# A two-block transformer forward pass on one core: GpSimd waits between its pieces, and the first stage's order changes

## What is computed

```
h = x @ w_in                    # 1024 x 2768: q_a, c_kv, q_idx, k_idx, w_idx, q_b, k_b, v_b, f_in
log_f = log_sigmoid(f_in + b_f);  cum_f = cumsum(log_f)
idx   = q_idx . k_idx                            # 8 index heads
score = sum_h w_idx[h] * relu(idx[h])            # causal, then top_k(64) per row
la = q_lat . c_kv[sel] + bias(t5_bucket)         # attention A, 8 heads, over the chosen keys
lb = q_b . k_b + cum_f[query] - cum_f[key]       # attention B, 8 heads, causal
y = concat(softmax(la) . c_kv @ w_uv, softmax(lb) . v_b) @ w_o
```

## Time and profile before

| | |
|---|---|
| median of 3 runs | 1362.13 us (1362.07 to 1362.14) |
| profiled execution | 1362.14 us, of which span 1360.8 us |
| PE busy | 1337.3 us, 98% |
| DVE busy | 1020.5 us, 75% |
| ACT busy | 783.5 us, 58% |
| POOL busy | 148.8 us, 11% |
| mean granted clock of TensorE | 0.998 |

### The profile page before, as it was taken

One profiled execution on the slowest core, in us unless ns is written; L12 is line 12 of the kernel. 1 busy time (PEld: TensorE's weight loads), 2 busy tenths in 40 slices (PEclk: granted clock), 3 DMA queues, 4 the chain that ended last, 5 costly groups with the idle time before them and its releaser, 6 DMA issues. The chain is left out here.

```text
span 1360.8 us, 20748 instructions
## 1 busy us (share of the span) xinstructions
PE 1337.3 (98%) x8197; PEld 1160.1 (85%) x8197; DVE 1020.5 (75%) x1681; ACT 783.5 (58%) x1268; POOL 148.8 (11%) x131
## 2 busy tenths in 40 slices
PE   7999999999999999999999999999999999999998
PEld 6987888888898788887986888888789998888887
DVE  5766478777896788778788677666567997786765
ACT  5644266665443565554677566555557875655553
POOL 4770300000100000000000000000302224000000
PEclk9999999999999999999999999999999999999999
DMA  8622165655563456553542255555344345455551
GB/s 302 244 78 124 65 228 209 242 198 188 193 243 129 182 190 227 196 196 124 211 167 96 97 214 215 216 188 191 148 158 183 127 154 186 151 190 204 193 197 72
DMA packets 38175, 242.17 MB, mean 178 GB/s; under 512 B 4416, under 2 KB 6848, under 8 KB 10688
## 3 DMA queue, kind: packets, MB, share of 16 engines
q1 hardware_dynamic: 38080, 240.86, 48.0%
HBM read 236.89 MB, written 2.64 MB: 176 GB/s over the span
## 5 line engine op out<-in xcount | busy, mean ns | idle before, releaser
L319 DVE TENSOR_TENSOR wlo<-raw,whi 128x2048 fp32r<-128x2048 f32 (+1 forms) x179 | 401.2, 2246 | 103.0 <-ACT whi L296 100.9
L296 ACT ACTIVATE whi<-raw 128x2048 fp32r<-128x2048 f32 x195 | 370.3, 1903 | 82.5 <-PE ps L471 40.0
L408 PE MATMUL ps<-XS,whi 128*128 128x512 f32 x1392 | 331.8, 390 | 0.0
L408 PEld LDWEIGHTS ps<-XS,whi 128*128 128x128 f32 x1392 | 257.8, 188 | 52.1 <-issue 0.6
L460 PE MATMUL ps<-whi,MS 128*128 128x512 f32 x960 | 233.5, 391 | 0.0
L460 PEld LDWEIGHTS ps<-whi,MS 128*128 128x128 f32 x960 | 177.5, 188 | 35.8 <-issue 0.4
L413 PEld LDWEIGHTS ps<-XS,wlo 128*128 128x128 f32 x1392 | 178.5, 191 | 6.8
L413 PE MATMUL ps<-XS,wlo 128*128 128x256 f32 x1392 | 180.6, 283 | 0.0
L388 PE MATMUL ps<-XS,whi 128*128 128x256 f32 x672 | 167.8, 290 | 0.0
L389 PE MATMUL ps<-XS,whi 128*128 128x256 f32 x672 | 164.1, 284 | 0.0
L304 POOL TENSOR_TENSOR wlo<-raw,whi 128x512 fp32r<-128x512 f32 x90 | 125.0, 1421 | 192.9 <-ACT whi L296 104.9
(11 more groups left out here) (330 smaller groups left out, 1543.8 us busy)
## 6 DMA issues: line engine op xcount, KB each, us to landing
raw<-in_up SPq DMA_DIRECT2D x88, 1024.0 KB, 4.8
raw<-in_down SPq DMA_DIRECT2D x44, 1024.0 KB, 4.9
raw<-in_hg_t SPq DMA_DIRECT2D x16, 1024.0 KB, 4.8
raw<-in_od_t SPq DMA_DIRECT2D x8, 1024.0 KB, 5.6
raw<-in_ev_a SPq DMA_DIRECT2D x6, 1024.0 KB, 9.7
raw<-in_wa_o SPq DMA_DIRECT2D x6, 1024.0 KB, 5.1
raw<-in_hg_o SPq DMA_DIRECT2D x6, 1024.0 KB, 4.8
raw<-in_ev_o SPq DMA_DIRECT2D x4, 1024.0 KB, 5.8
```

The costliest lines, as they stand in the source:

```text
L296: ac.activation(parts_of(m)[0][:, 0:w], raw[m % NRAW][:, 0:w], ACT.Copy).then_inc(w_hi)
L319: ve.tensor_tensor(lo[:, c], r[:, c], hi[:, c].bitcast(F32), ALU.subtract).then_inc(w_lo_v)
L408: pe.matmul(banks[i][:, 0:512], hi[:, c], XS[:, k, 0:512], start=(k == 0), stop=False)
```

## The change

GpSimd: between two pieces of 512 columns it now waits until the one before is complete (`pp`, a semaphore of its own), and before the first piece of a tile until its previous tile's low part is complete.

First stage: TensorE takes ev_a 3 between the index heads 0 to 3 and 4 to 7. ScalarE makes the high part of ev_a 5 between the Relus of heads 3 and 4, and that of ev_a 6 behind the Relu of head 7, where that of ev_a 5 was. The copies of L1403 and L1405 go from VectorE to ScalarE (`cum_rows_act`), one pair behind the copies of ev_a 4 (j = 0) and one behind those of ev_a 5 (j = 1). ScalarE waits there for the zero fills of KX (`e_zk`), of QX (`e_zq`) and for the running sum (`e_sn`). TensorE waits for 4 of `e_cum` and 4 of `e_own` before attention.

```diff
--- before.py
+++ after.py
@@ -299,10 +299,16 @@
             if m in PLACE and POOLT[m]:
                 r, (hi, lo), w = raw[m % NRAW], parts_of(m), SCHED[m][2]
                 po.wait_ge(w_hi, PLACE[m] + 1)
-                for a in range(0, w // 2 if SHARED[m] else w, 512):
+                if LOP[m] > 1:
+                    po.wait_ge(w_lo_p, LOP[m] - 1)
+                n = w // 2 if SHARED[m] else w
+                for a in range(0, n, 512):
+
+                    if a:
+                        po.wait_ge(pp.sem, pp.n)
                     c = slice(a, a + 512)
                     ins = po.tensor_tensor(lo[:, c], r[:, c], hi[:, c].bitcast(F32), ALU.subtract)
-                ins.then_inc(w_lo_p)
+                    ins.then_inc(w_lo_p if a + 512 == n else pp.up())
 
         def low_part_dve(m):
             if m in PLACE and (not POOLT[m] or SHARED[m]):
@@ -1103,6 +1109,7 @@
         ea, ev_, eb, ec, eo = FIRST["ev_a"], FIRST["ev_v"], FIRST["ev_b"], FIRST["ev_c"], FIRST["ev_o"]
         E0 = MS0["even"]
 
+        e_zk, e_zq, e_sn, e_own = mark("e_zk"), mark("e_zq"), mark("e_sn"), mark("e_own")
         AT_QB, AT_KB, AT_QA, AT_VB, AT_CT = [6, 8, 10, 12], [7, 9, 11, 15], [16, 17, 17, 18], 14, 5
 
         def x_ready(k):
@@ -1127,7 +1134,8 @@
                 ins = pe.transpose(bank[7][:, 16 * tt:16 * tt + 16], FW[0:16, 128 * tt:128 * tt + 128], ident[0:16, 0:16])
             ins.then_inc(e_fw.up())
             for h in range(0, 8, 2):
-
+                if h == 4:
+                    project(ea + 3, bank[4])
                 pe.wait_ge(e_ac.sem, 3 + h // 4)
                 if h >= 4:
                     pe.wait_ge(e_re.sem, h - 2)
@@ -1141,7 +1149,6 @@
                         ins = pe.matmul(bank[(h + r) % 4][:, a:b], QI[q, c:c + 128], KI[q, 0:b - a], start=True, stop=True)
                         if tt == 1:
                             ins.then_inc(e_ix.up())
-            project(ea + 3, bank[4])
             project(ea + 4, bank[5])
             project(ea + 5, bank[6])
             pe.wait_ge(e_wi.sem, 1)
@@ -1152,7 +1159,8 @@
             accumulate([ev_ + 1], XS, [4, 5, 6, 7], 512, acc, no_wait, False, True)
             pe.wait_ge(e_ac.sem, 6)
             project(eb, bank[4])
-            pe.wait_ge(e_cum.sem, 8)
+            pe.wait_ge(e_cum.sem, 4)
+            pe.wait_ge(e_own.sem, 4)
             pe.wait_ge(cb_in.sem, 1)
             for i in range(-2, 22):
                 if 0 <= i < 16:
@@ -1256,6 +1264,21 @@
                 pe.matmul(ePAIR[p % 2][64 * r:64 * r + 64, 0:256], WV[:, 64 * (h + r):64 * (h + r) + 64], OA[r], start=True,
                           stop=True).then_inc(e_po.up())
 
+        def cum_rows(r):
+            a = 64 - 64 * r
+            own = lambda p: ident[p:p + 8, p:p + 8].rearrange("p (c r) -> p c r", r=2)[:, :, r:r + 1].to_broadcast([8, 4, 256])
+            row = lambda ap: ap.unsqueeze(1).to_broadcast([8, 4, 256])
+            return a, a + 32, own, row
+
+        def cum_rows_act(r):
+
+            a, b, own, row = cum_rows(r)
+            ac.wait_ge(e_zk.sem, 2)
+            ac.activation(hx4(KX, r)[a:a + 8], own(a), ACT.Copy).then_inc(e_own.up())
+            ac.wait_ge(e_zq.sem, 2)
+            ac.wait_ge(e_sn.sem, 1)
+            ac.activation(hx4(QX, r)[a:a + 8], row(FW[a:a + 8, :]), ACT.Copy).then_inc(e_own.up())
+
         def even_act():
             def out_of(m, i, dst, scale=1.0):
                 ac.wait_ge(w_done, DONE[m])
@@ -1285,11 +1308,13 @@
                 ac.wait_ge(w_done, DONE[ea + 1 + j])
                 ac.activation(QI[:, 512 * j:512 * j + 512], bank[5 + j][:, :], ACT.Copy, scale=0.125).then_inc(e_ac.up())
             for h in range(8):
+                if h == 4:
+                    act_weights(ea + 5)
                 ac.wait_ge(e_ix.sem, h + 1)
                 if h >= 2:
                     ac.wait_ge(e_sc.sem, 2 * h - 2)
                 ac.activation(RR[h % 2], bank[h % 4][:, 0:384], ACT.Relu).then_inc(e_re.up())
-            act_weights(ea + 5)
+            act_weights(ea + 6)
             z = slice(0, 104)
             ac.wait_ge(e_fz.sem, 1)
             ac.wait_ge(e_fw.sem, 1)
@@ -1306,6 +1331,8 @@
                 act_weights(ea + 6 + j)
                 heads_of(ea + 4 + j, 0, KX, j)
                 heads_of(ea + 4 + j, 1, QX, j + 1, 0.125)
+                if j < 2:
+                    cum_rows_act(j)
             act_weights(ev_ + 3)
             for tt in range(2):
                 ac.wait_ge(w_done, DONE[ev_ + 1] - 1 + tt)
@@ -1348,7 +1375,7 @@
         def even_dve():
             ve.wait_ge(m_tp.sem, 4)
             for r in range(2):
-                ve.memset(hx4(KX, r)[64 - 64 * r:128 - 64 * r], 0.0).then_inc(dv.up())
+                ve.memset(hx4(KX, r)[64 - 64 * r:128 - 64 * r], 0.0).then_inc(e_zk.up())
             ve.wait_ge(e_fw.sem, 1)
             ve.tensor_scalar(WI, bank[7][:, 0:32], float(np.float32(8 ** -0.5)), None, ALU.mult).then_inc(e_wi.up())
             ve.wait_ge(e_wi.sem, 1)
@@ -1388,21 +1415,18 @@
             ve.wait_ge(e_ln.sem, 1)
             ve.tensor_tensor(FZ[z, :], FZ[z, :], FW[z, :], ALU.subtract).then_inc(dv.up())
             ve.wait_ge(dv.sem, dv.n)
-            ve.tensor_tensor_scan(FW[z, :], C("ones", 104), FZ[z, :], 0.0, ALU.mult, ALU.add).then_inc(dv.up())
-            ve.wait_ge(dv.sem, dv.n)
+            ve.tensor_tensor_scan(FW[z, :], C("ones", 104), FZ[z, :], 0.0, ALU.mult, ALU.add).then_inc(e_sn.up())
+            ve.wait_ge(e_sn.sem, 1)
             ve.wait_ge(d_skw, 16)
             for r in range(2):
-                ve.memset(hx4(QX, r)[64 - 64 * r:128 - 64 * r], 0.0).then_inc(dv.up())
+                ve.memset(hx4(QX, r)[64 - 64 * r:128 - 64 * r], 0.0).then_inc(e_zq.up())
             ve.tensor_scalar(FZ[z, :], FW[z, :], -1.0, None, ALU.mult).then_inc(dv.up())
             ve.wait_ge(dv.sem, dv.n)
+            ve.wait_ge(e_zk.sem, 2)
+            ve.wait_ge(e_zq.sem, 2)
             for r in range(2):
-                a = 64 - 64 * r
-                b = a + 32
-                own = lambda p: ident[p:p + 8, p:p + 8].rearrange("p (c r) -> p c r", r=2)[:, :, r:r + 1].to_broadcast([8, 4, 256])
-                row = lambda ap: ap.unsqueeze(1).to_broadcast([8, 4, 256])
-                ve.tensor_copy(hx4(QX, r)[a:a + 8], row(FW[a:a + 8, :])).then_inc(e_cum.up())
+                a, b, own, row = cum_rows(r)
                 ve.memset(hx4(QX, r)[b:b + 8], 1.0).then_inc(e_cum.up())
-                ve.tensor_copy(hx4(KX, r)[a:a + 8], own(a)).then_inc(e_cum.up())
                 ve.tensor_tensor(hx4(KX, r)[b:b + 8], own(b), row(FZ[b:b + 8, :]), ALU.mult).then_inc(e_cum.up())
             select(16)
             ve.wait_ge(dv.sem, dv.n)
```

## The result

The changed kernel takes 1366.28 us (median of 8 executions, 1364.61 to 1367.41); the kernel before, beside it on the same chip, takes 1362.45 us (8 executions, 1362.01 to 1365.48). The ratio is 1.0021, 95% interval 1.0013 to 1.0030: 3.8 us slower, where no difference was forecast. The profiled execution took 1366.79 us, its span is 1365.5 us (before: 1362.14 and 1360.8).

What follows compares the result with a forecast made beforehand. TensorE was taken as the bound, busy 1337.3 of 1360.8 us. Terms -1.1 (reordering), +0.2 (stall) and +0.6 (attention) gave -0.3 us against the profiled 1362.14, so 1361.8 us, range 1360.6 to 1363.6.

Steps and rivals of the forecast that it cites:

- Part 1: TensorE, first stage: with the fourth tile between heads 3 and 4, the fifth tile starts 1.1 us earlier.
- Part 2: ScalarE's order, first stage: Relus 4 to 7 keep the earlier rhythm, ev_a 6 split at 47.4, log-sigmoid work 4.7 us later.
- Part 3: VectorE, first stage: QX zero fills end at 57.4, 5.8 us of copies leave, selection ends some 1.5 us earlier, worth nothing.
- Part 4: ScalarE: four row copies of 1.0 us each; the first waits for the zero fill, first ev_v high part 4.0 us later.
- The stall: TensorE at the first ev_v tile's low part: a wait of 0.1 to 0.2 us.
- same: Whole kernel: no difference beyond 0.2%, 2.7 us, from the kernel before; chance 0.90.
- Part 5: GpSimd's waits for itself: 0.11 us per piece, 0.4 us per tile.
- later GpSimd tiles: GpSimd's tiles after attention begins: enough room for 0.4 to 0.8 us more, so cost 0.
- Attention: Start of attention: one more slow VectorE normalisation beside a GpSimd piece costs about 1.03 us, 0.6 counted.
- A: Rival: GpSimd becomes the bound with self-waits of 0.45 to 0.5 us a piece; +5.2 us, 1367.3 us, chance 0.07.
- C: Rival: ScalarE's wait for the zero fill is 2 us longer, first ev_v stall 1.9 us; +1.4, 1363.5 us, chance 0.13.

Runs made afterwards that it cites:

- Experiment 6: Changed kernel with GpSimd holding the low part of ev_a 5 until VectorE's weighted sum is done: 1366.83 us, ratio 1.0025 to the kernel before.
- experiment 3: Changed kernel with the first ev_v tile's split put first, ahead of the row copies on ScalarE: 1362.39 us, ratio 0.9994 to the kernel before.
- experiment 4: Changed kernel with the four row copies back on VectorE, all else as changed: 1365.5 us, ratio 1.0018 to the kernel before.
- experiment 1: Kernel before with only GpSimd's self-waits added: 1364.41 us, ratio 1.0009 to the kernel before.
- experiment 2: Changed kernel without GpSimd's self-waits: 1365.71 us, ratio 1.0019 to the kernel before; its profiled execution took 1363.43 us.
- experiment 8: More profiled executions: changed kernel without self-waits twice (1367.7, 1372.7 us); the same with ev_v split first and ev_a 5 held back once (1362.03 us).
- experiment 7: Changed kernel with ev_v split ahead of row copies and no self-waits: 1363.83 us (ratio 1.0014) with ev_a 5 held back, 1367.1 us (1.0015) without.
- experiment 9: Changed kernel, ev_v split first, self-waits only in tiles 9 to 12: 1362.64 us; everywhere but there: 1362.67 us; in all tiles: 1363.73 us.
- experiment 10: Changed kernel, ev_v split first, no self-waits, unused MAX8 added before the masks: one 1362.69 us, two 1362.94 us, none 1362.26 us.
- experiment 5: Kernel before and changed kernel, both unaltered, each profiled once more: 1365.38 and 1366.59 us.

## Why the prediction was wrong

**Part 1** was right: -1.03 us for -1.1, both L1141 waits gone.

**Part 2 is the step that failed.** It put the Relus 4 to 7 "in the rhythm of 0 to 3" and the split of ev_a 6 at 47.4, 10.9 us behind the small transposition. It came 13.1 behind it (48.24 - 35.12). The rhythm was read where GpSimd had no piece, and the same part moved a split forward that gave GpSimd pieces right there. The rows were in reach: the weighted sum's, and GpSimd's gap from 37.73 to 44.64. Experiment 6 gave the rhythm back by holding these pieces. Of the 2.2 us, about 1.3 are these pieces beside heads 4 to 7: in experiments 3 and 4, where the split of ev_a 5 came 3.5 behind the transposition, as forecast, that of ev_a 6 still came 12.3 behind. The other 0.9 go with the earlier pieces beside heads 0 to 3; both profiles of the changed kernel have them (ev_a 5 4.6 behind), neither of the kernel before.

**Parts 3 and 4** had the mechanism and the sizes apart from that: the row copies take 1.04 to 1.06 us each, forecast 1.0; ScalarE's wait for the zero fill is 2.27, forecast 2.0; the first ev_v split is "what is late next". Of its 2.6 us beyond the forecast (24.6 behind the transposition for 22.0) 2.2 are there by Part 2; of the rest, 0.2 is VectorE's two operations behind Abs (1.13 and 1.47 us for 1.01 and 1.40) and 0.2 is roundings in the fills and the copy (2.09 for 2.0, 1.08 for 1.0). From its start GpSimd then needed 6.29 us for the low part, forecast 6.4. The stall, forecast 0.1 to 0.2, was 2.33. With 0 to 0.3 us of room on three tiles in a row, a chance of 0.90 for "same" was too high: every delay of 1 us upstream was on the path.

**The clock** was not in the sum at all. Every stall was priced at its own length. Behind this one of 2.33 us TensorE's next tiles took 1.74 us more than in the kernel before, at a granted clock of 0.59 and 0.89, and behind experiment 1's of 2.40 us the clock was 0.60 from 41 to 45 us. After the wait of 1.1 us in experiment 2 it stayed at 1.00; of the two of 2.01 and 1.94 us (experiment 8) one was followed by 0.58, the other by 1.00.

**Part 5** was right in size: a tile of four pieces takes 5.44 us where nothing disturbs it, as the split-first kernel shows, against 5.01, 0.11 a piece.

```profile
93.81 5.44 POOL L310 TENSOR_TENSOR wlo<-raw,whi 128x512 fp32r<-128x512 f32 x4 [3.16 <-ACT whi L296]
```

It counted the self-waits as a price for nothing, but with the split first no kernel that had them showed a held or a long execution (0 of 44, for 21 of 59 without; experiments 7 to 10). It also put the later GpSimd tiles at 0, and one is not. After:

```profile
PE ps L2306 <- DVE ar L2570: 0.6, 1, 0.6
```

and before:

```profile
PE ps L2282 <- DVE ar L2546: 0.2, 1, 0.2
```

That is 0.35 us near 1142 us, and every profile with self-waits in all tiles has it. **Attention** cost 0.35 us of the 0.6, by the stage's sum, and not by one more long normalisation, which was put at 1.03: the waits for the normalisation were 1.7 us in two, the longest 1.3, and are 1.6 in four, the longest 0.4.

**Rivals.** A was off (no self-wait took 0.4 us). C was the one in place and size: against the transposition the zero fill came 2.5 us later than forecast, and the stall was 2.33. Its reason was another, though: it looked for the delay in the operations behind Ln, which gave 0.2, and not in the weighted sum. It gave 1363.5 us and a chance of 0.13; with the clock's 1.7 and the 0.35 it would have given 1365.6. The measured sum: -1.03 + 2.57 + 1.74 + 0.35 + 0.35 = +4.0 us, against 3.8 between the medians.

## What to carry to other kernels

Before an operation that waits is put into an engine's queue, look at what stands behind it and who needs that: here the same copies on the same engine cost over 3 us in front of a split and nothing that can be told behind it. A duration read from a trace holds for its neighbours; when the change moves another engine's work into that stretch, ask what it will run beside: the weighted sum took 0.35 us an operation with no piece of GpSimd's beside it and 0.61 with them. For a stall on TensorE of about 2 us reckon with two prices, its length and nearly twice that: both were measured here, 1.94 us with the clock at 1.00 behind it, and 2.33 us with 1.74 more. And time several executions before calling a wait useless, since what it may guard against came in one of three (21 of 59 executions over 1366 us).

## What the runs showed of the hardware

- One VectorE operation, the first of the masks (TENSOR_SCALAR 128x384), was held over many pieces of GpSimd's: 12.66, 8.97, 8.63 and 7.67 us for one of 0.36, beside ten, seven, seven and six pieces, in all four until 0.2 us after the end of GpSimd's run (experiments 8, 7, 10 and 8). In the kernel before it lasted 2.73 us, beside two pieces. In those four executions the top-8 operations just ahead of it, beside the same run of pieces, took what they took in the changed kernel: MAX8 0.43 and MATCH_REPLACE8 0.41 us for 128x256.
- Where GpSimd waited for its own last piece in that stretch, the operation lasted 1.50 us or less in all eight profiles. That the self-wait is what ends the hold is not shown: without it six of ten profiles of the new order had 1.49 us or less too. A tile of four pieces is 0.43 us longer by its self-waits (5.44 for 5.01).
- TensorE after a wait of 2.33 us (the changed kernel): granted clock 0.59 for 3.1 us, 0.89 for the next 4.1; after 2.01 (experiment 8): 0.58 for 2.8 us; after 1.94 (experiment 8) and after 1.1 (experiment 2): 1.00. After 2.29 us (the changed kernel again, experiment 5): 0.79 for 2.6 us, 0.72 for the next 4.1; after 2.31 (experiment 6): 0.76 and 0.74 for the same lengths; after 2.40 (experiment 1): 1.00 for 0.9 us, 0.60 for the next 4.0.
